# Two-layer decoder step on one core: the attention of layer 1 weighs its exponentials ahead of the value product, and collects the output as features by queries in one bank

## The chip, the cores and the metric

The program runs on one core of a Trainium2 chip. The metric is the device time of one launch in microseconds (us). TensorE is called PE here, VectorE DVE, ScalarE ACT, GpSimd POOL and SyncE SP, as the profile does. PSUM has eight banks of 512 fp32 columns per partition; the code calls them `PS[:, bank, :]`.

## What is computed

One step of a two-layer decoder trunk for a prompt of 512 tokens and 8 samples. Layer 1, which the change touches, is sparse attention with 16 query heads in 4 groups (one K/V head each). For the prompt it comes down to:

```python
o_c, p_c = cmp_attend(q, q_pos, blocks)        # 16 block means as keys
o_s = sel_attend(q_rot, q_pos, idx, rows)      # chosen 64-token blocks
o_w = win_attend(q_rot, q_pos, kv_w, k_pos)    # window of 512
gate = sigmoid(gts + b_gate)                   # 3 per head and query
o = gate[..., 0:1] * o_c + gate[..., 1:2] * o_s + gate[..., 2:3] * o_w
y = einsum('bte,ed->btd', o.reshape(B, T, NSA_W) * silu(z), w_out)
```

With 512 tokens there are 8 blocks and the top 16 are taken, so the selected branch is plain causal attention over its own K/V, as is the window branch. Each branch is a softmax of its own.

## The kernel before

Every projection is a tile of 128 output features by 520 columns (512 prompt tokens and 8 samples). `project` multiplies it with fp32 data split in a high and a low part: for each of 16 slices k of the contraction, three products (high by high, low by high, high by low) of two halves of 260 columns, six matmuls. ACT makes the high part of the weights (`split_hi`, `split_half`), POOL the low part (`split_lo`, four operations of 128x512 for a tile), and the weights come in by SP's queue, two tiles ahead. All layers together have some 145 such tiles.

Layer 1 goes through the 4 groups `g`, unrolled. A group has 14 tiles: 4 of queries, 6 of keys and values (with the samples' paged caches worked in between), and 4 of z, the output gate, one for each head `jj`. Beside the four z tiles stand the 16 **turns** n of the prompt's attention: `jj = n // 4` is the head, `i = n % 4` the block of 128 queries, and with i the number of key blocks grows from 1 to 4, for the selected (r = 0) and the window branch (r = 1). The engines are in-order queues with semaphores, the order is the code's. In turn n PE

- waits for the exponentials of turn n (`at_exp`), turns them (`T`, a multiplication with the identity; i + 1 blocks for each branch) into banks 4 and 5,
- multiplies the scores of turn n + 1 into banks 0 and 1 (`scores`), and runs 2 to 5 slices k of the z tile (`project(... part=...)`),
- turns back the combined output of turn n - 1 (`back`),
- in even turns 2 to 12 multiplies values of a sample's cache (`values`), whose sum DVE takes out (`d_vs`, awaited by the next turn's transposes),
- and multiplies the turned exponentials with the values of both branches and the compressed one, each into 128 columns of its own in bank 6 + n % 2: queries by features.

DVE in turn n copies the turned window part to SBUF, then adds the mask and takes the maxima of turn n + 1 (`maxima`), makes gate over sum for turn n (`weight`), copies the turned-back output of turn n - 1 (`backed`), takes out sample sums or the z tile, and adds the three products of turn n, each weighed by a number per query (`combine`). After a head, `gated` multiplies by silu(z). ACT copies the turned selected part, takes the exponentials of turn n + 1 with their sums (`expo`), and at the end of each head silu, with table loads; after `expo` in turns 4, 5, 8, 9, 12 and 13 it makes half of a tile's high part. POOL's four operations follow the second half.

In group 3 the splits of the output (`y_hi`, `y_lo`) for the output projection stand in turns 12 to 15 and behind them. The output projection's first tile waits for them slice by slice. `end_of_group` stands behind the first four slices of the tile that follows a group.

Of the kernel before, what the change touches and what calls it, by code (L numbers as in the profile page):

```python
# [18 lines left out]
ALU = mybir.AluOpType  # L19
AX = mybir.AxisListType.X  # L20

P = 128
D = 2048
KT = D // P
TP, NS = 512, 8
# [129 lines left out]
def trunk(nc, I, O):  # L155
    ctx = ExitStack()
    with ctx:
# [84 lines left out]
        weighed = few[:, 1024:1152], S1["pnb"]  # L242
# [558 lines left out]
        def _(pe):  # L801
# [195 lines left out]
            for g in range(4):  # L997
# [142 lines left out]
                def back(n, g=g):  # L1140

                    pe.wait_ge(S["at_cb"], 16 * g + (n + 1))
                    T(PS[:, 6 + n % 2, 384:512], weighed[n % 2], ident).then_inc(S["at_bk"], 1)

# [39 lines left out]
                for n in range(16):  # L1184
                    jj, i = n // 4, n % 4
                    pe.wait_ge(S["at_exp"], 16 * g + (n + 1))
# [27 lines left out]
                    if n >= 2:  # L1214
                        pe.wait_ge(S["at_be"], 16 * g + (n - 1))
                    to = 6 + n % 2
                    for s in range(i + 1):
                        M(PS[:, to, 0:P], lhsT=pt[:, 0, s * P:(s + 1) * P], rhs=vr[:, 0, s * P:(s + 1) * P],
                          start=(s == 0), stop=(s == i))
                    pe.wait_ge(S["at_ptb"], 16 * g + (n + 1))  # L1220
                    for s in range(i + 1):
                        M(PS[:, to, P:2 * P], lhsT=pt[:, 1, s * P:(s + 1) * P], rhs=vr[:, 1, s * P:(s + 1) * P],
                          start=False, stop=(s == i), skip_group_check=True)
                    if n == 0:
                        pe.wait_ge(S["a_ptc"], g + 1)
# [4 lines left out]
                def end_of_group(g=g, back=back):  # L1230

                    back(15)
                    pe.wait_ge(S["a_rd"], 2 * g + 2)
# [299 lines left out]
        def _(dve):  # L1533
# [282 lines left out]
            for g in range(4):  # L1816
# [127 lines left out]

                def combine(n):

                    w, ot, of = st[:, 6 + n % 2], weighed[n % 2], PS[:, 6 + n % 2]
                    dve.wait_ge(S["at_o"], 16 * g + (n + 1))
                    step(TS(ot, of[:, 0:P], w[:, 0:1], None, ALU.mult))
                    step(STT(ot, of[:, P:2 * P], w[:, 1:2], ot, ALU.mult, ALU.add))  # L1950
                    TT(ot, ot, of[:, 2 * P:3 * P], ALU.add).then_inc(S["at_cb"], 1); own.done("at_cb")

                def backed(n):

                    jj, i = n // 4, n % 4
                    if g == 0 and n == 0:
                        dve.wait_ge(S["x_saved"], 32)
                    dve.wait_ge(S["at_bk"], 16 * g + (n + 1))
                    CPR(XY[:, bass.ds(4 * g + jj, 1), i * P:(i + 1) * P], PS[:, 6 + n % 2:7 + n % 2, 384:512]
                        ).then_inc(S["at_be"], 1); own.done("at_be")  # L1960

                def gated(jj):
# [18 lines left out]
                step(ins)  # L1981
                dve.wait_ge(S["d_eT"], g + 1)
# [27 lines left out]
                for n in range(16):  # L2010
# [9 lines left out]
                    if n:  # L2020
                        if i == 3:
                            t = Tile(A_BASE, 10 + jj, g, 14)
                            dve.wait_ge(S["proj_done"], t.n + 1)
# [4 lines left out]
                    if g == 3 and n == 15:  # L2028
                        y_lo(dve, own, 1, range(4, 6))
# [77 lines left out]
```

## Time and profile before

| | |
|---|---|
| median of 3 runs | 2167.11 us (2166.88 to 2167.21) |
| profiled execution, its time | 2167.76 us |
| its span, first to last instruction | 2166.0 us |
| PE busy with matmuls | 2134.1 us, 99% |
| DVE busy | 881.6 us, 41% |
| ACT busy | 703.8 us, 32% |
| POOL busy | 761.4 us, 35% |
| granted TensorE clock, mean | 0.999 |

Busy times are sums of instructions over the span. An in-order engine that is busy 41% of the time can still keep another waiting, so the wait rows of single places count here, not the shares. In a timeline row the first number is the start, the second the time from the first start to the last end of a run of like instructions. One fp32 product of the code stands as two passes on PE, one transpose as one. The time of a matmul includes its way through the array, so starts, not ends, tell how closely they follow. A number like 2.53 us for two instructions that overlap is not their sum.

### The profile page before, as it was taken

What the parts mean: (1) busy time and instruction counts of PE and PEld (TensorE: products, weight loads), DVE (VectorE), ACT (ScalarE), POOL (GpSimd) and SP (SyncE); (2) the same over time, 40 slices, a digit from 0 to 9 for tenths busy, and PEclk for the clock granted to TensorE, in tenths of its full rate; (3) what the DMA queues carried; (4) which work ended last, traced back from release to release, by engine and by line L of the source; (5) the groups of instructions that cost most, each with busy time, mean ns of one, the idle gap of its engine ahead of it and who ended that gap; (6) DMA issues with size and microseconds to landing.
All of it is one profiled execution on the core that took longest, in us unless ns stands there. A gap on an engine that the chain in (4) does not pass through costs nothing. (4 is left out here: it accounts for less than half of the span.)

```text
span 2166.0 us, 43620 instructions
## 1 busy us (share of the span) xinstructions
PE 2134.1 (99%) x17971; PEld 2031.3 (94%) x17971; DVE 881.6 (41%) x1831; ACT 703.8 (32%) x983; POOL 761.4 (35%) x584
## 2 busy tenths in 40 slices
PE   8999999999999999999999999999999999999998
PEld 7999999989899899999889999899898999899998
DVE  6423225135351462134356532663346532664112
ACT  5212124232242342142234322442234322444223
POOL 2444433425334344444321243214331242223441
PEclk9999999999999999999999999999999999999999
DMA  7333555637556334455534344344634345333433
GB/s 256 93 98 88 178 156 128 189 97 188 152 130 185 98 98 123 139 178 165 158 103 123 99 128 132 106 115 109 164 105 123 99 125 134 100 102 99 121 103 109
DMA packets 455224, 281.17 MB, mean 130 GB/s; under 512 B 19224, under 2 KB 445784, under 8 KB 453747
## 3 DMA queue, kind: packets, MB, share of 16 engines
q1 hardware_dynamic: 455051, 278.73, 45.8%
q8 instruction: 125, 2.05, 0.4%
q14 instruction: 48, 0.39, 0.1%
HBM read 249.87 MB, written 45.99 MB: 137 GB/s over the span
## 5 line engine op out<-in xcount | busy, mean ns | idle before, releaser
L345 POOL TENSOR_TENSOR w_lo<-w_raw,w_hi 128x512 fp32r<-128x512 f32 (+1 forms) x580 | 761.2, 1343 | 1371.0 <-ACT w_hi L329 1029.0
L368 PE MATMUL ps<-h_hi,w_hi 128*128 128x260 f32 x4640 | 962.8, 289 | 7.3 <-DVE h_lo L460 7.2
L368 PE MATMUL ps<-h_hi,w_lo 128*128 128x260 f32 x4640 | 934.4, 283 | 0.0
L368 PE MATMUL ps<-h_lo,w_hi 128*128 128x260 f32 x4640 | 932.8, 283 | 0.0
L368 PEld LDWEIGHTS ps<-h_hi,w_hi 128*128 128x128 f32 x4640 | 717.9, 188 | 31.5 <-issue 17.0
L368 PEld LDWEIGHTS ps<-h_hi,w_lo 128*128 128x128 f32 x4640 | 713.8, 188 | 0.0
L368 PEld LDWEIGHTS ps<-h_lo,w_hi 128*128 128x128 f32 x4640 | 712.5, 188 | 0.0
L329 ACT ACTIVATE w_hi<-w_raw 128x2048 fp32r<-128x2048 f32 x132 | 251.9, 1909 | 519.8 <-PE ps L368 497.5
L432 DVE TENSOR_TENSOR scratch<-ps,rstd 128x520 f32<-128x520 f32 x48 | 33.6, 700 | 265.9 <-PE ps L368 265.3
L469 DVE TENSOR_TENSOR xy<-ps,x_res 128x520 f32<-128x520 f32 x32 | 22.4, 700 | 256.1 <-PE ps L368 253.5
L1461 ACT ACTIVATE scratch<-ps,scratch 128x128 f32<-128x128 f32 (+3 forms) x128 | 66.3, 523 | 125.5 <-DVE scratch L1933 125.1
L501 ACT ACTIVATE scratch<-xy 128x520 f32 (+1 forms) x32 | 20.4, 638 | 256.0 <-DVE xy L469 247.3
L1448 ACT ACTIVATE rstd<-ps 64x520 f32<-64x520 f32 x24 | 14.4, 602 | 207.2 <-PE ps L368 207.2
L1120 PE MATMUL ps<-scratch 128*128 128x128 f32 (+3 forms) x256 | 80.0, 435 | 0.0
L1900 DVE TENSOR_TENSOR scratch<-ps,scratch 128x520 f32<-128x520 f32 x16 | 11.2, 700 | 113.8 <-ACT rstd L1449 113.8
L388 ACT ACT_TABLE_LOAD x44 | 56.5, 1283 | 1.5 <-PEq L2093 0.7
L1120 PEld LDWEIGHTS ps<-scratch 128*128 128x128 f32 x256 | 41.1, 191 | 16.1 <-issue 11.0
L1819 DVE COPY scratch<-ps 128x512 f32<-128x512 f32 x32 | 22.1, 692 | 80.4 <-PE ps L1019 79.9
L1473 ACT ACTIVATE scratch<-ps 128x128 f32<-128x128 f32 (+1 forms) x64 | 28.0, 437 | 79.5 <-PE ps L1193 79.0
L1932 DVE TENSOR_REDUCE scratch<-ps 128x2 f32<-128x256 f32 (+1 forms) x64 | 52.8, 825 | 2.2
L1193 PE MATMUL ps<-c_common,scratch 128*128 128x128 f32 x320 | 45.7, 274 | 4.3 <-ACT scratch L1461 4.2
L1761 DVE SCALAR_TENSOR_TENSOR scratch<-scratch 128x256 f32<-128x256 f32 x64 | 48.4, 756 | 2.3
(363 smaller groups left out, 1760.6 us busy)
## 6 DMA issues: line engine op xcount, KB each, us to landing
w_raw<-in_w_in SPq DMA_DIRECT2D x113, 1024.0 KB, 5.8
w_raw<-in_w_out SPq DMA_DIRECT2D x32, 1024.0 KB, 5.9
scratch<-in_cache_kv_sel SPq DMA_DIRECT2D x256, 64.0 KB, 1.9
scratch<-in_cache_kv_win SPq DMA_DIRECT2D x128, 128.0 KB, 2.4
scratch<-in_cache_kv_cmp SPq DMA_DIRECT2D x256, 64.0 KB, 2.0
out_kvw_s<-in_cache_kv_win SPq DMA_DIRECT2D x24, 512.0 KB, 6.7
x_scratch<-xy SPq DMA_DIRECT2D x2, 4160.0 KB, 14.5
x_res<-x_scratch SPq DMA_DIRECT2D x32, 260.0 KB, 6.1
```

What stands on the lines that cost most here:

```text
L329: nc.scalar.activation(WH[:, t.p, :, n], WR[:, t.p, :, n], ACT.Copy).then_inc(S["w_hi"], 1); own.done("w_hi")
L345: ins = nc.gpsimd.tensor_tensor(WL[:, t.p, k:k + 4, 0:n], WR[:, t.p, k:k + 4, 0:n], WH[:, t.p, k:k + 4, 0:n].bitcast(F32), ALU.subtract)
L368: mm = nc.tensor.matmul(PS[0:m, bank + c, 0:HALF], lhsT=w[:, t.p, k, 0:m], rhs=h[:, k, c * HALF:(c + 1) * HALF], start=(k == 0 and x == 0) ...
L388: own.step(nc.scalar.activation(CELL[:], ones[0:1, 0:1], func))
L432: ins = nc.vector.tensor_tensor(halves(out), ps2(t), halves(RS[:]), ALU.mult)
L469: nc.vector.tensor_tensor(halves(XY[:, 2 * i + j, :]), ps2(t), halves(XR[:, j]), ALU.add).then_inc(proj_read[t.p], 1)
L1120: mm = M(PS[:, r, 0:(i + 1) * P], lhsT=qt[:, jj, i * P:(i + 1) * P], rhs=kT[:, r, 0:(i + 1) * P], start=True, stop=True)
L1193: mm = T(PS[:, 4 + r, s * P:(s + 1) * P], pr[:, 2 * (n % 2) + r, s * P:(s + 1) * P], ident)
L1461: ins = A(pr[:, 2 * (n % 2) + r, 0:L], PS[:, r, 0:L], ACT.Exp, bias=S1["st"][:, 4 + n % 2, r:r + 1], scale=SCALE, accum_out=S1["st"][:, n ...
L1473: A(pt[:, 0, 0:L], PS[:, 4, 0:L], ACT.Copy).then_inc(S["at_pta"], 1); own.done("at_pta")
L1761: STT(cb[:, b, c * HD:(c + 1) * HD], S0["vb"][:, b], KDW[:, c, b:b + 1], cb[:, b, c * HD:(c + 1) * HD], ALU.mult, ALU.add).then_inc(S["m_c ...
L1932: step(V.tensor_reduce(st[:, 2 + n % 2], PS[:, 0:2, 0:(i + 1) * P], AX, ALU.max))
```

## The change

`weight(n)` now also multiplies the exponentials of both branches by gate over sum, in place, in SBUF (two operations of 128 x (i + 1)·128), and tells `at_w`; PE's transposes wait for that instead of `at_exp`. It is called for the turn ahead, `weight(n + 1)` in turn n, and `weight(0)` ahead of the group's compressed softmax. In the value product stationary and moving sides change places: values stand, weighed and turned exponentials move, so the result is features by queries, and all branches of the four query blocks of a head add up in the 512 columns of one bank (6 + jj % 2). The compressed branch is one product of 512 columns at a head's start. `combine`, `back` and `backed` go away; `gated` reads the bank. `end_of_group` waits for `gated(3)`. In group 3 one of the output's splits moves ahead.

```diff
@@ TensorE, a turn
-                    pe.wait_ge(S["at_exp"], 16 * g + (n + 1))
+                    pe.wait_ge(S["at_w"], 16 * g + (n + 1))
...
-                        back(n - 1)
...
-                    if n >= 2:
-                        pe.wait_ge(S["at_be"], 16 * g + (n - 1))
-                    to = 6 + n % 2
+                    to = 6 + jj % 2
+                    if i == 0:
+                        if n == 0:
+                            pe.wait_ge(S["a_ptc"], g + 1)
+                        if jj >= 2:
+                            pe.wait_ge(S["a_yz"], 4 * g + jj - 1)
+                        M(PS[:, to, :], lhsT=S1["vzf"][:, jj], rhs=few[:, 0:TP], start=True, stop=False,
+                          skip_group_check=True)
                     for s in range(i + 1):
-                        M(PS[:, to, 0:P], lhsT=pt[:, 0, s * P:(s + 1) * P], rhs=vr[:, 0, s * P:(s + 1) * P],
-                          start=(s == 0), stop=(s == i))
+                        M(PS[:, to, i * P:(i + 1) * P], lhsT=vr[:, 0, s * P:(s + 1) * P], rhs=pt[:, 0, s * P:(s + 1) * P],
+                          start=False, stop=False, skip_group_check=True)
...
-                    M(PS[:, to, 2 * P:3 * P], lhsT=few[:, i * P:(i + 1) * P], rhs=S1["vzf"][:, jj],
-                      start=False, stop=True, skip_group_check=True).then_inc(S["at_o"], 1)
+                    mm.then_inc(S["at_o"], 1)
...
-                    back(15)
+                    pe.wait_ge(S["a_yz"], 4 * g + 4)
@@ VectorE
+                    for r in range(2):
+                        p = pr[:, 2 * (n % 2) + r, 0:(i + 1) * P]
+                        ins = TS(p, p, st[:, 6 + n % 2, r:r + 1], None, ALU.mult)
+                    ins.then_inc(S["at_w"], 1); own.done("at_w")
...
-                def combine(n):
-
-                    w, ot, of = st[:, 6 + n % 2], weighed[n % 2], PS[:, 6 + n % 2]
-                    dve.wait_ge(S["at_o"], 16 * g + (n + 1))
-                    step(TS(ot, of[:, 0:P], w[:, 0:1], None, ALU.mult))
-                    step(STT(ot, of[:, P:2 * P], w[:, 1:2], ot, ALU.mult, ALU.add))
-                    TT(ot, ot, of[:, 2 * P:3 * P], ALU.add).then_inc(S["at_cb"], 1); own.done("at_cb")
-
-                def backed(n):
...
                 def gated(jj):
...
-                    y = XY[:, bass.ds(4 * g + jj, 1), 0:TP]
-                    TT(y, y, XR[:, jj % 2:jj % 2 + 1, 0:TP], ALU.mult)
+                    TT(XY[:, 4 * g + jj, 0:TP], PS[:, 6 + jj % 2, :], XR[:, jj % 2, 0:TP], ALU.mult)
...
                 step(ins)
+                weight(0)
                 dve.wait_ge(S["d_eT"], g + 1)
...
                     if n < 15:
                         maxima(n + 1)
-                    weight(n)
+                    if n > 0 and i == 0:
+                        gated(jj - 1)
+                    if n < 15:
+                        weight(n + 1)
                     if g == 3 and n in (13, 14):
                         y_lo(dve, own, 1, range(2 * n - 26, 2 * n - 24))
...
                     if g == 3 and n == 15:
-                        y_lo(dve, own, 1, range(4, 6))
+                        y_lo(dve, own, 1, range(4, 7))
...
-                    combine(n)
...
                 if g == 3:
-                    y_lo(dve, own, 1, range(6, 10))
-                backed(15)
+                    y_lo(dve, own, 1, range(7, 10))
                 gated(3)
```

Line numbers of the rows that follow are those of each kernel's own file. DVE's queue at the start of a group's turns, before (L1978 is the last operation on the samples' new keys, L1983 the copy that PE's transposes of turn 0 wait for, L1988 the start of the compressed softmax):

```order
L1974 COPY scratch<-ps 128x256
L1975 TENSOR_TENSOR scratch<-ps,scratch 64x512
L1978 TENSOR_TENSOR scratch<-ps,scratch 128x32 x2
L1983 COPY scratch<-ps 128x128
L1988 TENSOR_TENSOR scratch<-ps,scratch 128x64 x4
```

And of the changed kernel:

```order
L1959 COPY scratch<-ps 128x256
L1960 TENSOR_TENSOR scratch<-ps,scratch 64x512
L1963 TENSOR_TENSOR scratch<-ps,scratch 128x32 x2
L1936 RECIPROCAL scratch<-scratch 128x2
L1937 TENSOR_TENSOR scratch<-scratch 128x2
L1942 TENSOR_SCALAR scratch<-scratch 128x128 x2
L1969 COPY scratch<-ps 128x128
L1974 TENSOR_TENSOR scratch<-ps,scratch 128x64 x4
```

`weight(0)`, four operations, now stands ahead of that copy and of the whole compressed softmax.

DVE's queue in turns 1 and 2, before, from the copy of the turned exponentials of turn 1 (L1930 to L1933 are `maxima`, L1940 and L1941 `weight`, L1550 `backed`, L1949 to L1951 `combine`):

```order
L2014 COPY scratch<-ps 128x256
L1930 TENSOR_TENSOR ps<-ps,scratch 128x128 x2
L1932 TENSOR_REDUCE scratch<-ps 128x2
L1933 TENSOR_SCALAR scratch<-scratch 128x2
L1940 RECIPROCAL scratch<-scratch 128x2
L1941 TENSOR_TENSOR scratch<-scratch 128x2
L1550 TENSOR_SCALAR xy<-ps 128x128
L1949 TENSOR_SCALAR scratch<-ps,scratch 128x128
L1950 SCALAR_TENSOR_TENSOR scratch<-ps,scratch 128x128
L1951 TENSOR_TENSOR scratch<-scratch,ps 128x128
L2014 COPY scratch<-ps 128x384
```

And of the changed kernel, the same two turns, to the sample sum that ends turn 2 (L2025):

```order
L2000 COPY scratch<-ps 128x256
L1926 TENSOR_TENSOR ps<-ps,scratch 128x128 x2
L1928 TENSOR_REDUCE scratch<-ps 128x2
L1929 TENSOR_SCALAR scratch<-scratch 128x2
L1936 RECIPROCAL scratch<-scratch 128x2
L1937 TENSOR_TENSOR scratch<-scratch 128x2
L1942 TENSOR_SCALAR scratch<-scratch 128x384 x2
L2000 COPY scratch<-ps 128x384
L1926 TENSOR_TENSOR ps<-ps,scratch 128x128 x2
L1928 TENSOR_REDUCE scratch<-ps 128x2
L1929 TENSOR_SCALAR scratch<-scratch 128x2
L1936 RECIPROCAL scratch<-scratch 128x2
L1937 TENSOR_TENSOR scratch<-scratch 128x2
L1942 TENSOR_SCALAR scratch<-scratch 128x512 x2
L2025 COPY rstd<-ps 128x128
```

The four operations of 128x128 are gone; the two in place (L1942) are between the maxima and the next turn's copy, and in turn 2 ahead of the sample sum.

PE's queue in turns 0 and 1, before, from the last slice of turn 0 (L1218 and L1222 are the value products, L1226 the compressed one, L1193 the transposes, L1120 the scores):

```order
L368 MATMUL ps<-h_hi,w_lo 128x260 x2
L1218 MATMUL ps<-scratch 128x128
L1222 MATMUL ps<-scratch 128x128
L1226 MATMUL ps<-scratch 128x128
L1193 MATMUL ps<-c_common,scratch 128x128 x4
L1120 MATMUL ps<-scratch 128x384 x2
```

And of the changed kernel:

```order
L367 MATMUL ps<-h_hi,w_lo 128x260 x2
L1213 MATMUL ps<-scratch 128x512
L1216 MATMUL ps<-scratch 128x128
L1220 MATMUL ps<-scratch 128x128
L1187 MATMUL ps<-c_common,scratch 128x128 x4
L1119 MATMUL ps<-scratch 128x384 x2
```

The compressed product moved ahead of the turn's value products and is four times as wide.

## Rows read from the trace of the kernel before

**Rows 1.** The page, busy time of engines: us, share of the span, instructions.

```profile
PE 2134.1 (99%) x17971; PEld 2031.3 (94%) x17971; DVE 881.6 (41%) x1831; ACT 703.8 (32%) x983; POOL 761.4 (35%) x584
```

**Rows 2.** The waits from 1100 us on: total, times, longest (us).

```profile
PE ps L1193 <- ACT scratch L1461: 4.2, 4, 1.1
```

**Rows 3.** Timeline of PE, group 0, turns 0 to 6: start, us, instruction.

```profile
1122.92 0.38 PE L1193 MATMUL ps<-c_common,scratch 128*128 128x128 f32 x2
...
1130.11 0.66 PE L1193 MATMUL ps<-c_common,scratch 128*128 128x128 f32 x4 [0.96 <-ACT scratch L1461]
...
1134.05 0.27 PE L1143 MATMUL ps<-c_common,scratch 128*128 128x128 f32 x1
1134.16 0.61 PE L1218 MATMUL ps<-scratch 128*128 128x128 f32 x4
...
1135.28 0.84 PE L1193 MATMUL ps<-c_common,scratch 128*128 128x128 f32 x6
...
1142.00 1.04 PE L1193 MATMUL ps<-c_common,scratch 128*128 128x128 f32 x8
...
1146.86 0.38 PE L1193 MATMUL ps<-c_common,scratch 128*128 128x128 f32 x2
...
1159.35 0.82 PE L1193 MATMUL ps<-c_common,scratch 128*128 128x128 f32 x6
```

**Rows 4.** Timeline of ACT: the last part of the exponentials of turns 2, 3, 4, 6.

```profile
1134.99 0.20 ACT L1461 ACTIVATION_READ_ACCUMULATOR scratch<-ps,scratch 128x1 f32 x1
...
1141.25 0.20 ACT L1461 ACTIVATION_READ_ACCUMULATOR scratch<-ps,scratch 128x1 f32 x1
...
1145.95 0.20 ACT L1461 ACTIVATION_READ_ACCUMULATOR scratch<-ps,scratch 128x1 f32 x1
...
1157.82 0.20 ACT L1461 ACTIVATION_READ_ACCUMULATOR scratch<-ps,scratch 128x1 f32 x1
```

**Rows 5.** Timeline of DVE, group 0, turns 0 and 2.

```profile
1122.05 0.27 DVE L1978 TENSOR_TENSOR scratch<-ps,scratch 128x32 f32<-128x32 f32 x2
1122.46 0.29 DVE L1983 COPY scratch<-ps 128x128 f32<-128x128 f32 x1
...
1133.90 0.17 DVE L1940 RECIPROCAL scratch<-scratch 128x2 f32<-128x2 f32 x1
1134.10 0.16 DVE L1941 TENSOR_TENSOR scratch<-scratch 128x2 f32<-128x2 f32 x1
...
1140.66 0.29 DVE L2038 COPY rstd<-ps 128x128 f32<-128x128 f32 x1
```

**Rows 6.** Timeline of DVE before the turns: products by a number per partition, SBUF to SBUF.

```profile
1115.78 0.29 DVE L1874 TENSOR_SCALAR scratch<-c_common,scratch 128x128 f32<-128x128 f32 x1
1115.98 0.35 DVE L1875 TENSOR_SCALAR scratch<-scratch 128x256 f32<-128x256 f32 x1
```

**Rows 7.** DVE's groups by form: count, busy us, mean ns, idle before.

```profile
L1668 DVE TENSOR_SCALAR scratch<-scratch 128x384 f32<-128x384 f32 x4 | 1.7, 421 | 0.1
```

**Rows 8.** Timeline of POOL and DVE near 1107 and 1118 us.

```profile
1107.29 2.53 POOL L345 TENSOR_TENSOR w_lo<-w_raw,w_hi 128x512 fp32r<-128x512 f32 x2 [9.06 <-ACT w_hi L329]
1107.44 1.16 DVE L1906 COPY scratch<-scratch 128x8 f32<-128x8 f32 x1
...
1118.21 5.01 POOL L345 TENSOR_TENSOR w_lo<-w_raw,w_hi 128x512 fp32r<-128x512 f32 x4 [5.90 <-ACT w_hi L329]
```

**Rows 9.** Timeline of group 3, turns 13 and 15: the output's splits beside POOL.

```profile
1942.65 1.43 DVE L460 TENSOR_TENSOR h_lo<-xy,h_hi 128x520 fp32r<-128x520 f32 x2
...
1943.35 0.20 ACT L1461 ACTIVATION_READ_ACCUMULATOR scratch<-ps,scratch 128x1 f32 x1
...
1944.71 4.99 POOL L345 TENSOR_TENSOR w_lo<-w_raw,w_hi 128x512 fp32r<-128x512 f32 x4 [21.22 <-ACT w_hi L337]
...
1960.05 6.31 DVE L460 TENSOR_TENSOR h_lo<-xy,h_hi 128x520 fp32r<-128x520 f32 x4
```

**Rows 10.** Timeline of POOL in turn 6.

```profile
1159.18 1.27 POOL L345 TENSOR_TENSOR w_lo<-w_raw,w_hi 128x512 fp32r<-128x512 f32 x1 [35.96 <-ACT w_hi L337]
```

More of the change, by code:

```diff
@@ L1138, in cmp_turn @@
                     mm.then_inc(S["a_ctT"], 1)
-                def back(n, g=g):
-                    pe.wait_ge(S["at_cb"], 16 * g + (n + 1))
-                    T(PS[:, 6 + n % 2, 384:512], weighed[n % 2], ident).then_inc(S["at_bk"], 1)
                 def values(s):
@@ L1213, in _, with end_of_group @@
                         sample_rows(range(4))
[L1214 to L1216 removed]
+                    to = 6 + jj % 2
[6 more added lines that the diff above has]
+                          skip_group_check=True)
                     for s in range(i + 1):
[L1218 to L1219 removed]
+                        M(PS[:, to, i * P:(i + 1) * P], lhsT=vr[:, 0, s * P:(s + 1) * P], rhs=pt[:, 0, s * P:(s + 1) * P],
+                          start=False, stop=False, skip_group_check=True)
                     pe.wait_ge(S["at_ptb"], 16 * g + (n + 1))
                     for s in range(i + 1):
[L1222 to L1225, printed above, removed]
[L1226 to L1227 removed]
+                        mm = M(PS[:, to, i * P:(i + 1) * P], lhsT=vr[:, 1, s * P:(s + 1) * P],
+                               rhs=pt[:, 1, s * P:(s + 1) * P], start=False, stop=(i == 3 and s == i),
+                               skip_group_check=True)
+                    mm.then_inc(S["at_o"], 1)
                 sample_rows(range(4, 6))
[L1230 to L1232 removed]
+                def end_of_group(g=g):
+                    pe.wait_ge(S["a_yz"], 4 * g + 4)
                     pe.wait_ge(S["a_rd"], 2 * g + 2)
@@ L1943, in weight, with gated @@
                             S1["gw"][:, bass.ds(12 * g + (3 * jj + 1), 2), i:i + 1], ALU.mult))
-                def combine(n):
-                    w, ot, of = st[:, 6 + n % 2], weighed[n % 2], PS[:, 6 + n % 2]
-                    dve.wait_ge(S["at_o"], 16 * g + (n + 1))
-                    step(TS(ot, of[:, 0:P], w[:, 0:1], None, ALU.mult))
-                    step(STT(ot, of[:, P:2 * P], w[:, 1:2], ot, ALU.mult, ALU.add))
-                    TT(ot, ot, of[:, 2 * P:3 * P], ALU.add).then_inc(S["at_cb"], 1); own.done("at_cb")
-                def backed(n):
-                    jj, i = n // 4, n % 4
-                    if g == 0 and n == 0:
+                    for r in range(2):
+                        p = pr[:, 2 * (n % 2) + r, 0:(i + 1) * P]
+                        ins = TS(p, p, st[:, 6 + n % 2, r:r + 1], None, ALU.mult)
+                    ins.then_inc(S["at_w"], 1); own.done("at_w")
+                def gated(jj):
+                    if g == 0 and jj == 0:
                         dve.wait_ge(S["x_saved"], 32)
[L1958 to L1962, printed above, removed]
+                    dve.wait_ge(S["at_o"], 16 * g + 4 * jj + 4)
                     dve.wait_ge(S["a_z"], 4 * g + jj + 1)
-                    y = XY[:, bass.ds(4 * g + jj, 1), 0:TP]
-                    TT(y, y, XR[:, jj % 2:jj % 2 + 1, 0:TP], ALU.mult)
+                    TT(XY[:, 4 * g + jj, 0:TP], PS[:, 6 + jj % 2, :], XR[:, jj % 2, 0:TP], ALU.mult)
                     CP(S1["zs"][:, jj:jj + 1], XR[:, jj % 2:jj % 2 + 1, TP:TA]).then_inc(S["a_yz"], 1)
@@ L2044, in _ @@
                            ).then_inc(S["a_rd"], 1); own.done("a_rd")
-                    if n > 0 and i == 0:
-                        gated(jj - 1)
-                    combine(n)
                 dve.wait_ge(S["a_rdT"], 2 * g + 2)
```

15 lines of the change are left out of this document (6 added, 9 removed).

## The prediction

> **What bounds the kernel now.** I read the busy shares first: PE is busy 99% of the span [rows 1], so whatever leaves PE's queue shortens the time, and whatever makes PE wait lengthens it one for one. Then the waits of the part that the change touches: PE waits there for one thing only, the exponentials, four times, 4.2 us in all [rows 2], once per group, in turn 1 [rows 3]. Then the timeline, for how near the other turns are to such a wait. I compare the start of PE's transposes with the end of the exponentials that they need [rows 3, 4]: turn 1 waits; turn 2 starts at 1135.28, and its exponentials ended at 1134.99 + 0.20 = 1135.19, so it has 0.09 us to spare; turn 3 has 1142.00 - 1141.45 = 0.55; turn 4 has 1146.86 - 1146.15 = 0.71; turn 6 has 1159.35 - 1158.02 = 1.33. Every group repeats this. So the exponentials of the first turns, where only 2 or 3 slices of projection stand between scores and transposes, are on the path already, though DVE is busy 41%.
>
> **What the change takes off PE.** 64 turns back. One costs the distance of its start from the next one's, 1134.16 - 1134.05 = 0.11 us [rows 3]. The compressed products keep their columns: four of 128 (two passes each of 0.11 us, 0.22 a turn) become one of 512 (two passes of four times 0.11 or slightly less, about 0.87). The value products keep count and columns. So PE's own work falls by 64 x 0.11 = 7.0 us, 7.3 with the compressed part; within a head three turns get 0.33 shorter and the first 0.5 longer.
>
> **What it adds ahead of the transposes.** `weight` now stands between exponentials and transposes. Reciprocal and small product stand 0.20 us apart each [rows 5]. The products in place: 128 columns take 0.29 us with the next one 0.20 behind, 256 take 0.35 [rows 6], 384 take 0.42 [rows 7]; 0.07 per 128 columns, so 512 take 0.49 (estimate). The second starts about 0.08 us before the first has ended, as in [rows 6]. With about 0.10 to get from ACT to DVE (I take it from the neighbouring starts) and the same last step to PE as before, the transposes start after the end of the exponentials by 0.10 + 0.40 + first + last + 0.05: 1.04, 1.17, 1.31 and 1.45 us for 128 to 512 columns, where before 0.05 would do.
>
> **Turn by turn, group 0.** From the start of one turn's transposes to the next:
>
> - Turn 1 to 2: before 1135.28 - 1130.11 = 5.17. Now exponentials end 1135.19 - 1130.11 = 5.08 after the start of turn 1, as they hang on PE's scores and not on what is removed, then 1.31: 6.39. **+1.2**.
> - Turn 2 to 3: before 6.72. Exponentials 1141.45 - 1135.28 = 6.17, then 1.45; and here the sample sum is queued behind the products in place, and the transposes of turn 3 wait for it too: +0.3 (L2038 of [rows 5]), where before it was done long ahead. 7.94. **+1.2**.
> - Turn 3 to 4: before 4.86. Exponentials 4.15; 0.25 of it was DVE still in `combine`; 3.90 + 1.04 = 4.94. **+0.1**.
> - Turns 0 and 1: `weight(0)` stands ahead of the copy that PE awaits and of the compressed softmax, which DVE goes through without a pause until the maxima of turn 1. L1978 ends at 1122.32. The reciprocal ends at 1122.53. The small product reads two operands from SBUF, and POOL is in its four operations until 1118.21 + 5.01 = 1123.22 [rows 8]. That such a DVE operation waits for the running POOL one shows at 1107.44: a copy of 8 columns took 1.16 us, until the first of POOL's (2.53 / 2 = 1.26 us each) was over [rows 8]. So it ends near 1123.30, the products in place at 1123.83, and the copy starts at 1123.86 instead of 1122.46 [rows 5]: 1.40 late. All of it reaches turn 1's exponentials (before: end at 1130.06, the wait's end in [rows 3]), which then need 1.17: 1130.06 + 1.40 + 1.17 = 1132.63 against 1130.11. **+2.5**. The wider compressed product lies in this wait.
> - Turns 4 to 15: the spare time is 0.7 to 2.5 us, about what `weight` wants. Where PE decides, a head gets 4 x 0.11 + 0.02 shorter; the first turns of heads 2 to 4 begin about 0.1 late, as turn 4, and turns 6, 10, 14 are at par (1.33 against 1.31). I book **-0.1** for the twelve turns: PE's saving, given back in these places.
>
> A group comes to 1.2 + 1.2 + 0.1 + 2.5 - 0.1 = **+4.9 us**, four of them +19.6.
>
> **Group 3** has the output's low parts (L460) behind `weight` in turns 13 and 14. Before, two of them ran at 1942.65 and took 1.43 [rows 9], just ahead of POOL at 1944.71. Now they come behind `weight(14)`: exponentials end at 1943.55, products in place end 1.36 to 1.4 later, 1944.94, when POOL has started or stands first in line. Beside POOL four of them took 6.31, 1.58 each [rows 9]. The transposes of turn 14 wait for a copy behind them. I take 1944.94 + 1.3 + 0.6 + 1.7 + 0.75 = about 1949.2, against 1945.3 + 0.3 that the other groups pay: +3.5 more than these (+1.5 if DVE gets in first). Turn 15: two more, 1.43, behind `weight(15)` and ahead of the sample sum: +1.5. At the end PE now waits at the fifth slice for `gated(3)`, which stands behind three low parts beside POOL, where before it waited piecemeal at later slices for the same low parts: +0.3. Together +5.3.
>
> **Sum**: +19.6 + 5.3 = +24.9 us. The profiled execution took 2167.76 with a span of 2166.0; the median of the runs is 2167.11, 0.65 below it. On the median: 2167.1 + 24.9 = **2192**.
>
> **The lock, by the Trainium skill.** The Trainium skill (SBUF — State Buffer, Who interferes with whom) says that DVE and GpSimd share a pair of ports, that a DVE operation on two SBUF tensors, or a single-source one in a two-port mode, takes it exclusively, and that who issues first blocks the other for the whole instruction. The 1.16 us copy agrees. By that rule the products in place, 128 of them, are all of the kind that can be caught, and turn 0 is where they are; where DVE comes first, POOL waits, and that costs nothing.
>
> **Rivals.**
>
> (1) *PE's saving carries, no new waits* (faster): `weight` would have to lie in spare time everywhere: -7.3 us, **2160**. It speaks for it that PE is 99% busy and DVE loses 256 operations; against it that turns 1 to 3 have 0, 0.09 and 0.55 us to spare [rows 3, 4] and cannot hide 1.2 to 1.5. It decides only if `weight` cost under 0.3 us. Chance 5%.
>
> (2) *The chain is about half as long as I make it*, say 0.6 us a turn, no lock in turn 0, low parts in time: group +1.9 rather than +4.9, group 3 +1: about +9, **2176**. 10%.
>
> (3) *The lock catches more turns.* In turns 6, 10 and 14 POOL starts 1159.18 - 1158.02 = 1.16 us after the exponentials end [rows 4, 10]; the second product in place should start 0.10 + 0.40 + 0.34 = 0.84 after it. The margin is 0.32. If it is lost, each of 12 turns waits up to 1.25 us more: +15, **2207**. 10%.
>
> (4) *No net change*: saving and waits cancel, within 4.3 us (0.2%) of 2167. It needs waits of 7 us in all, 1.8 a group, less than turns 2 and 3 alone give. 3%.
>
> The forecast itself has 72%, and its own spread is 2182 to 2200: 0.2 us of error in `weight` at 16 waiting places is 3.2, the lock in turn 0 (0.6 x 4) 2.4, group 3's race 2 to 3.5. With the cases around it the range is 2175 to 2204. Faster by over 0.2% (what a measurement can tell from no change): 0.06; within: 0.04; slower: 0.90.
>
> **What the profile after would show.** PE's busy time some 7 us less, no turning back, and PE's waits for DVE's products in place (they can appear as waits for DVE `scratch` at the transposes) of about 1.2 us or more at turns 1, 2 and 3 of every group; the copy ahead of turn 0 near 1.4 us later in its group, with a small product of 128x2 lasting about 0.7; in group 3 a wait of 3 us at turn 14. Wrong I would be if the transposes of turns 2 and 3 start within 0.5 us of their exponentials' end, or if the exponentials come earlier than 5.08 and 6.17 us behind the turn before, which would mean that `combine` had delayed them.

## The result and the profile after

The changed kernel takes 2199.07 us (median of 4 runs, 2197.93 to 2199.52) against 2167.11: ratio 1.0146, 95% interval 1.0134 to 1.0158, slower by 32.0 us. The forecast was 2192, range 2175 to 2204. The profiled execution has a span of 2197.3 us, 31.3 more than before, and a mean granted clock of 0.997.

The page's busy times, to set beside [rows 1]:

```profile
PE 2137.2 (97%) x17811; PEld 2019.7 (92%) x17811; DVE 841.0 (38%) x1703; ACT 704.1 (32%) x983; POOL 761.5 (35%) x584
```

DVE is 41 us less busy and PE has 160 instructions fewer, yet the kernel is slower: PE's share fell from 99 to 97%. PE's busy time did not fall by the removed 7 us; it rose by 3. Stretches at half clock (below) are part of that, but not most: experiment 3, whose mean clock is 0.999 again, still has 2135.1, and experiment 6, where the new waits are gone, 2125.4. So the time has to be looked for in PE's waits, from 1100 us on (total, times, longest), beside the one row of [rows 2] (the short ones, 0.6 us and less in total, are left out):

```profile
PE ps L1187 <- DVE scratch L1942: 13.5, 21, 1.4
PE ps L1187 <- DVE rstd L2025: 5.9, 4, 1.5
PE ps L1187 <- DVE scratch L2030: 4.7, 4, 3.7
PE ps L1187 <- DVE scratch L1969: 4.3, 4, 1.1
PE ps L367 <- DVE scratch L1952: 3.9, 1, 3.9
PE ps L1187 <- DVE scratch L2019: 1.5, 1, 1.5
```

All are waits for DVE. L1187 are the transposes. L1942 are the products in place, L2025 the sample sum queued behind them in turn 2, L1969 the copy ahead of turn 0, L2030 the copy of sample rows in turn 13, L2019 a sample sum in turn 14, L1952 the end of `gated(3)`. Together 33.8 us. The kernel before had the 4.2 of [rows 2] and one row more, which [rows 2] leaves out: PE waits for low parts at the end of group 3.

```profile
PE ps L368 <- DVE h_lo L460: 3.2, 3, 1.7
```

So about 26 us of the waits are new, not 30.

PE's timeline in group 0 (start, us, instruction, wait), to set beside [rows 3]:

```profile
1123.74 0.44 PE L1187 MATMUL ps<-c_common,scratch 128*128 128x128 f32 x2 [1.07 <-DVE scratch L1969]
...
1132.26 0.66 PE L1187 MATMUL ps<-c_common,scratch 128*128 128x128 f32 x4 [0.93 <-DVE scratch L1942]
...
1138.64 0.88 PE L1187 MATMUL ps<-c_common,scratch 128*128 128x128 f32 x6 [1.39 <-DVE scratch L1942]
...
1146.69 1.06 PE L1187 MATMUL ps<-c_common,scratch 128*128 128x128 f32 x8 [1.47 <-DVE rstd L2025]
...
1151.68 0.44 PE L1187 MATMUL ps<-c_common,scratch 128*128 128x128 f32 x2 [0.28 <-DVE scratch L1942]
```

Turns 1 to 4 each begin with a wait. From turn 1 to 2 it is 1138.64 - 1132.26 = 6.38 us (forecast 6.39), to turn 3 8.05 (7.94), to turn 4 4.99 (4.94). DVE's timeline at the same places:

```profile
1121.97 0.17 DVE L1936 RECIPROCAL scratch<-scratch 128x2 f32<-128x2 f32 x1
1122.17 0.67 DVE L1937 TENSOR_TENSOR scratch<-scratch 128x2 f32<-128x2 f32 x1
1122.87 0.48 DVE L1942 TENSOR_SCALAR scratch<-scratch 128x128 f32<-128x128 f32 x2
1123.39 0.29 DVE L1969 COPY scratch<-ps 128x128 f32<-128x128 f32 x1
...
1137.44 0.17 DVE L1936 RECIPROCAL scratch<-scratch 128x2 f32<-128x2 f32 x1 [1.43 <-ACT scratch L1457]
1137.64 0.16 DVE L1937 TENSOR_TENSOR scratch<-scratch 128x2 f32<-128x2 f32 x1
1137.84 0.75 DVE L1942 TENSOR_SCALAR scratch<-scratch 128x384 f32<-128x384 f32 x2
```

DVE is idle 1.43 us until the exponentials of turn 2 end, then runs `weight` in 1.15, and the transposes start 0.05 later, at 1138.64. In turn 0 the small product took 0.67 instead of 0.16: POOL was in its four operations until 1122.82, and the product ended at 1122.84. The other three groups show the same, 0.67 or 0.68.

Group 3, turns 13 and 14, is the other place. The timeline of POOL, DVE and PE, to set beside [rows 9]:

```profile
1966.18 0.75 DVE L1942 TENSOR_SCALAR scratch<-scratch 128x384 f32<-128x384 f32 x2
...
1966.86 5.86 POOL L344 TENSOR_TENSOR w_lo<-w_raw,w_hi 128x512 fp32r<-128x512 f32 x4 [21.37 <-ACT w_hi L336]
...
1966.97 3.39 DVE L459 TENSOR_TENSOR h_lo<-xy,h_hi 128x520 fp32r<-128x520 f32 x2
1970.39 0.68 DVE L2030 COPY scratch<-ps 8x512 f32<-8x512 f32 x1
...
1971.22 1.50 PE L1187 MATMUL ps<-c_common,scratch 128*128 128x128 f32 x6 [3.74 <-DVE scratch L2030]
1972.51 2.95 PE L1119 MATMUL ps<-scratch 128*128 128x512 f32 x4
```

The two low parts took 3.39 us instead of 1.43, with POOL's operations between them, and the copy behind them came late. A thing I had not expected is in the last two rows: six transposes in 1.50 us (0.82 to 0.88 elsewhere) and the scores in 2.95 (1.88 elsewhere). PE's clock had fallen. The windows of that place, and those of the end of the group (stretch; busy us of PE, PEld, DVE, ACT, POOL; granted clock; DMA share; GB/s):

```profile
1967.00:1971.00 4.00, 0.48 (x5) 0.29 (x3) 3.93 (x3) 1.72 (x3) 4.00 (x3) 1.00 0.00 0
1971.00:1975.00 4.00, 3.78 (x11) 2.46 (x11) 0.63 (x2) 0.49 (x1) 1.71 (x2) 0.57 0.00 0
1975.00:1979.00 4.00, 4.00 (x34) 3.76 (x33) 1.89 (x4) 1.38 (x4) 0.00 (x0) 1.00 0.00 0
...
1993.00:1997.00 4.00, 3.45 (x16) 3.45 (x17) 3.83 (x7) 2.06 (x4) 1.71 (x2) 0.50 0.52 154
1997.00:2001.00 4.00, 4.00 (x29) 4.00 (x29) 2.65 (x5) 0.49 (x1) 0.00 (x0) 0.81 1.15 312
```

Twice PE waited nearly 4 us and then ran at the 1.2 GHz level (0.50) for 3 to 5 us. PE's rows at the end of the group, the first behind the wait and the last of the slow stretch:

```profile
1993.55 0.80 PE L367 MATMUL ps<-h_hi,w_hi 128*128 128x260 f32 x2 [3.87 <-DVE scratch L1952]
...
1998.48 0.44 PE L367 MATMUL ps<-h_hi,w_lo 128*128 128x260 f32 x2
```

Pairs of slices' matmuls stand 0.43 us apart until 1998.48 and 0.24 after it: from 1993.55 on eleven distances took 4.93 us instead of 2.64, 2.3 more.

### The profile page after: what moved, and what is told of

Read it like the earlier page. It is cut to its first block and busy times, and to the rows that moved or that the text cites. A ratio compares the mean times of both kernels' runs of the same rounds, so it can differ in the third digit from the quotient of the medians.

```text
span 2197.3 us, 43028 instructions
## 1 busy us (share of the span) xinstructions
PE 2137.2 (97%) x17811; PEld 2019.7 (92%) x17811; DVE 841.0 (38%) x1703; ACT 704.1 (32%) x983; POOL 761.5 (35%) x584
## 5 line engine op out<-in xcount | busy, mean ns | idle before, releaser
L1187 PE MATMUL ps<-c_common,scratch 128*128 128x128 f32 x320 | 48.2, 282 | 29.8 <-DVE scratch L1942 13.5
L1187 PEld LDWEIGHTS ps<-c_common,scratch 128*128 128x128 f32 x320 | 35.4, 142 | 37.5 <-DVE scratch L1942 24.0
L2000 DVE COPY scratch<-ps 128x128 f32<-128x128 f32 (+1 forms) x64 | 31.4, 491 | 62.1 <-PE ps L1187 61.3
```

Source lines behind the costliest of these rows:

```text
L1187: mm = T(PS[:, 4 + r, s * P:(s + 1) * P], pr[:, 2 * (n % 2) + r, s * P:(s + 1) * P], ident)
L2000: CP(pt[:, 1, 0:L], PS[:, 5, 0:L]).then_inc(S["at_ptb"], 1); own.done("at_ptb")
```

## The experiments

Each ratio is to runs of the kernel before on the same chip (median 2167.35 for experiments 1 to 4, 2167.21 for 5 to 8). Where a difference to the changed kernel is given, it is to its 2199.07, which stands beside 2167.11.

**1. No weighing ahead of the transposes.** PE waits for the exponentials again, and the products in place are gone (so the output is not weighed).

```diff
-                    pe.wait_ge(S["at_w"], 16 * g + (n + 1))
+                    pe.wait_ge(S["at_exp"], 16 * g + (n + 1))
...
-                    for r in range(2):
-                        p = pr[:, 2 * (n % 2) + r, 0:(i + 1) * P]
-                        ins = TS(p, p, st[:, 6 + n % 2, r:r + 1], None, ALU.mult)
-                    ins.then_inc(S["at_w"], 1); own.done("at_w")
```

Expected:

> The changed kernel without the products in place: PE's transposes wait for the exponentials alone, as before, and the exponentials stay unweighed (gate and sum are left out of the output); all else, the product's orientation, the wide compressed product and the queues' order, is as changed. My theory (the time is lost in the chain from exponentials over weight to the transposes): turns 2 and 3 start within 0.1 us of the before's distance or earlier, what is left is PE's saving of about 7 us, against about 0.9 us a group from the small operations of weight(0) ahead of the copy, and about 3 us at the end of group 3: about 2166 us (2161 to 2171). Rival one, the product itself got slower on PE (its orientation, 512 columns at once): 2190 or more. Rival two, DVE and POOL block each other all over: also most of it gone, but then turns far from POOL's bursts would have shown no wait.

Measured: 2172.47 us, ratio 1.0021 (1.0012 to 1.0031). 26.6 of the 32 us are gone, so the weighing is the cause in the main. The expected 2166 was not reached, and the waits tell why:

```profile
PE ps L367 <- DVE scratch L1948: 3.9, 1, 3.9
PE ps L1187 <- DVE rstd L2021: 2.2, 4, 0.6
PE ps L1187 <- DVE scratch L1965: 2.2, 4, 0.5
PE ps L1187 <- DVE scratch L2026: 2.1, 1, 2.1
```

What is left are the small operations of `weight` (waits at turns 0 and 3) and group 3: the low parts are still in front of what PE awaits, turn 13 to 14 is 1.9 longer than before, 14 to 15 2.1, and the end, which waits 3.9 again, 1.2. Of the 2.1, 1.7 are PE's clock: behind the wait of 2.1 us at turn 14 the granted clock was 0.74 from 1945 to 1947 us and 0.50 from 1947 to 1949, and the exponentials of turn 15 ended 7.2 us after the transposes of turn 14 (5.5 in the other groups). The other groups are 0.4 to 0.7 us shorter each than before, where I had booked PE's whole saving, 1.8.

**2. The numbers, but not the products.** The wait stays, at the small product of `weight`; the two products in place are left out (the output is not weighed).

```diff
-                    step(TT(st[:, 6 + n % 2:7 + n % 2].rearrange("p o r -> p r o"),
+                    TT(st[:, 6 + n % 2:7 + n % 2].rearrange("p o r -> p r o"),
...
-                            S1["gw"][:, bass.ds(12 * g + (3 * jj + 1), 2), i:i + 1], ALU.mult))
-                    for r in range(2):
-                        p = pr[:, 2 * (n % 2) + r, 0:(i + 1) * P]
-                        ins = TS(p, p, st[:, 6 + n % 2, r:r + 1], None, ALU.mult)
-                    ins.then_inc(S["at_w"], 1); own.done("at_w")
+                            S1["gw"][:, bass.ds(12 * g + (3 * jj + 1), 2), i:i + 1], ALU.mult).then_inc(S["at_w"], 1); own.done("at_w")
```

Expected:

> As the run without weighing, but the transposes wait for reciprocal and small product (gate over sum), which are not applied (the output is unweighed). My theory: 0.5 us more at turns 1 and 2, about 0.7 at turn 3 (the sample sum is queued behind), next to nothing elsewhere, so about 1.6 us a group over the run without weighing: about 2172 us (2168 to 2177). If the products in place alone were the cost, it would equal the run without weighing.

Measured, in one run, so without an interval: 2176.37 us. Waiting for the reciprocal and the small product costs 3.9 us over experiment 1 (expected about 6: turn 3 came no later, since it waits for the sample sum in both), the products in place the other 22.7. The small ones alone are waited for in turns 1 and 2 only, the turns with nothing to spare:

```profile
PE ps L1187 <- DVE scratch L1937: 4.4, 8, 0.6
```

With the products it is turns 4, 8 and 12 too, and the sample sum and the copy behind them.

**3. Low parts behind what PE waits for.** In group 3 the splits of turns 13 and 14 move behind the copy of the sample rows, and the last three behind `gated(3)`. Nothing else changes.

```diff
                     if n < 15:
                         weight(n + 1)
-                    if g == 3 and n in (13, 14):
-                        y_lo(dve, own, 1, range(2 * n - 26, 2 * n - 24))
...
                            ).then_inc(S["a_rd"], 1); own.done("a_rd")
+                    if g == 3 and n in (13, 14):
+                        y_lo(dve, own, 1, range(2 * n - 26, 2 * n - 24))
...
-                if g == 3:
-                    y_lo(dve, own, 1, range(7, 10))
                 gated(3)
...
+                if g == 3:
+                    y_lo(dve, own, 1, range(7, 10))
```

Expected:

> The changed kernel with group 3's low parts (y_lo) behind what PE waits for: in turns 13 and 14 behind the copy and the sample sum, at the end behind gated(3). My theory: turn 14 and 15 start as in the other groups (10.55 becomes about 7.1, 11.06 about 7.9 us), the granted clock stays at 1.00 there, and PE's wait of 3.9 us at the end goes back to the 3 us that the kernel before has in pieces: 9 to 11 us less, about 2189 us (2186 to 2193). Rival, the waits of group 3 only hide others (PE waits there for the same thing anyway): under 3 us less.

Measured: 2189.73 us, ratio 1.0103 (1.0086 to 1.0120), 9.3 less than the changed kernel. That is group 3's own share. From turn 13 to 14 it gives back 3.4 us, from 14 to 15 2.6, and from turn 15 to the end 4.0; the last is 1.2 more than the change had cost there, because the kernel before also waits for low parts at that place (10.0 in sum; turn 0 of group 3 came 0.4 later in this execution). What PE waits for at the end now, and the windows of both places, where the clock stays up:

```profile
PE ps L367 <- DVE h_lo L459: 2.0, 2, 1.3
```

```profile
1968.00:1972.00 4.00, 3.72 (x22) 2.80 (x23) 3.85 (x6) 1.74 (x3) 4.00 (x4) 1.00 0.00 0
1984.00:1988.00 4.00, 2.61 (x19) 2.32 (x19) 3.90 (x4) 3.13 (x6) 4.00 (x4) 1.00 0.48 139
1988.00:1992.00 4.00, 3.27 (x27) 3.06 (x26) 3.83 (x6) 0.12 (x1) 0.28 (x1) 1.00 1.15 315
```

The same low parts beside the same POOL burst: with nobody waiting for what stands behind them they cost nothing from turn 13 to 14 (7.14 us, 7.13 in the other groups), and 0.5 from 14 to 15. The 13.5 us of waits for the products in place are untouched.

**4. Scores ahead of the transposes.** PE multiplies the scores of turn n + 1 as soon as the exponentials of turn n are done, while DVE weighs them; DVE takes the maxima of turn n + 1 ahead of the copy of the turned part.

```diff
+                    pe.wait_ge(S["at_exp"], 16 * g + (n + 1))
+                    if n < 15:
+                        scores(n + 1)
                     pe.wait_ge(S["at_w"], 16 * g + (n + 1))
...
                     mm.then_inc(S["at_T"], 1)
-                    if n < 15:
-                        scores(n + 1)
...
+                    if n < 15:
+                        maxima(n + 1)
                     dve.wait_ge(S["at_T"], 16 * g + (n + 1))
                     CP(pt[:, 1, 0:L], PS[:, 5, 0:L]).then_inc(S["at_ptb"], 1); own.done("at_ptb")
-                    if n < 15:
-                        maxima(n + 1)
```

Expected:

> The changed kernel with PE's scores of the next turn ahead of its transposes (they need only the end of the exponentials, not the weighing), and DVE's maxima ahead of the copy of the turned part, so that the scores' 0.4 to 1.8 us lie in the time of the weighing. My theory: turns 1, 2, 3 lose 1.2, 1.5 and 1.6 us each of their distance, turns 4, 8, 12 about 0.3: 4 to 5.5 us a group, 16 to 22 in all, about 2180 us (2176 to 2184). Rival (PE's own work grew): within 3 us of 2199.

Measured: 2168.41 us, ratio 1.0004 (0.9995 to 1.0014): 30.7 us less than the changed kernel, where I had expected about 19. It does more than cover `weight`. Turn 1 to 2 is 5.20 us again, but 2 to 3 is 5.63, less than before (6.72): the exponentials of the next turn no longer hang on the transposes and DVE's copy of them, so they end 3.3 us after the transposes of turn 1 instead of 5.08, and 3.8 after those of turn 2 instead of 6.20. The first three groups are 0.8 to 1.1 us shorter than before, 6.5 shorter each than in the changed kernel. Group 3 gains 5.2 more than these: its wait at turn 14 fell from 3.74 us to 1.59, the granted clock stayed at 1.00 behind it, and turn 14 to 15 took 6.61 us instead of 11.06. What is left, the largest rows:

```profile
PE ps L1119 <- DVE scratch L1970: 4.2, 4, 1.1
PE ps L367 <- DVE scratch L1953: 3.9, 1, 3.9
PE ps L1190 <- DVE scratch L2031: 1.6, 1, 1.6
```

The start of a group (L1970, the copy behind `weight(0)`), and group 3; 1.5 us more are the sample sum at turn 3. Behind the 3.9 us at the end the clock is down again (0.52 from 1961 to 1965 us).

**5. Both, and one wait later.** Experiments 3 and 4 together; the wait for that copy (`d_ptd`) moves from ahead of turn 0 to behind its scores.

```diff
-                pe.wait_ge(S["d_ptd"], g + 1)
                 for n in range(16):
...
                     pe.wait_ge(S["at_w"], 16 * g + (n + 1))
+                    if n == 0:
+                        pe.wait_ge(S["d_ptd"], g + 1)
```

Expected:

> Both repairs in one kernel: scores ahead of the transposes, low parts behind what PE waits for; the wait for the copy at a group's start also moves behind the first scores. If the two are independent, the second takes off the 9.3 us here too: 2168.4 - 9.3 = about 2159 us (2156 to 2162), faster than the kernel before, so that PE's saving of 7 us shows in the end. If PE waits for the same thing in both, less: 2163 or more. The moved wait gives at most 0.9 us a group, and I expect nothing of it, since the turn of the compressed softmax is awaited next.

Measured: 2163.49 us, ratio 0.9983 (0.9974 to 0.9992). Below the kernel before by 0.2%, 4.9 us less than experiment 4, where 9.3 had been the worth of the low parts alone. Moving them gave 3.4, 2.6 and 4.0 us from turn 13 to 14, from 14 to 15 and at the end in experiment 3; on top of experiment 4 it gives 1.8, nothing and 3.9, since the slack of the new order already takes up much of what the low parts delay. The two gains overlap, as the second reading of the expectation had it. At the start of the groups a new wait shows in place of the old one:

```profile
PE ps L1133 <- DVE scratch L1995: 3.3, 4, 0.9
...
PE ps L1191 <- DVE scratch L1971: 1.1, 4, 0.3
```

L1133 turns the compressed probabilities, which DVE finishes behind `weight(0)` (L1995 is their last operation).

**6. The start of a group too.** The copy that turn 0 awaits goes ahead of `weight(0)`; DVE takes the maxima of turn 1 ahead of the compressed softmax and weighs turn 1 within it; PE turns the compressed probabilities in turn 1 and adds their product in the third turn of a head. ACT's exponentials of turn 1 move ahead of the compressed ones with them. One bank for all branches is what makes the late product possible: it may come at any place of the sum.

```diff
-                weight(0)
                 dve.wait_ge(S["d_eT"], g + 1)
                 CP(S1["ptc2"].rearrange("p a b -> p (a b)"), PS[:, 4, 0:128]).then_inc(S["d_ptd"], 1)
                 own.done("d_ptd")
+                weight(0)
+                maxima(1)
...
-                    if i == 0:
-                        if n == 0:
+                    if i == 0 and jj >= 2:
+                        pe.wait_ge(S["a_yz"], 4 * g + jj - 1)
+                    if i == 2:
+                        if n == 2:
                             pe.wait_ge(S["a_ptc"], g + 1)
...
-                        M(PS[:, to, :], lhsT=S1["vzf"][:, jj], rhs=few[:, 0:TP], start=True, stop=False,
+                        M(PS[:, to, :], lhsT=S1["vzf"][:, jj], rhs=few[:, 0:TP], start=False, stop=False,
```

Expected:

> As the kernel with both repairs, and the group's start reordered: DVE takes the maxima of turn 1 and copies turn 0 ahead of the compressed softmax, weighs turn 1 in the middle of it, PE turns the compressed part in turn 1 and multiplies it in as a head's third turn. My theory (DVE's unbroken chain from weight(0) over the compressed softmax to the exponentials of turn 1 costs 2.0 us a group after the change): turn 1's transposes 2 to 3 us earlier, 1 to 2 us of it kept: about 2153 us (2150 to 2157). Rival: the chain only moves to turn 2's exponentials: within 1 us of the kernel with both repairs.

Measured: 2155.50 us, ratio 0.9947 (0.9933 to 0.9960), 11.7 below the kernel before and 43.6 below the changed one. Its page, and its longest waits:

```profile
PE 2125.4 (99%) x17811; PEld 2013.2 (93%) x17811; DVE 842.5 (39%) x1703; ACT 704.2 (33%) x983; POOL 760.7 (35%) x584
```

```profile
PE ps L367 <- DVE h_lo L459: 2.0, 2, 1.3
PE ps L1119 <- ACT scratch L1461: 0.6, 4, 0.2
```

PE is busy 8.7 us less than before: here the saving of the change (7.3 by the forecast) shows at last, with no wait longer than 0.2 us in the turns.

**7. Control: the same order on the kernel before.** Scores ahead of the transposes, maxima ahead of the copy, the wait for the first copy behind the scores; the old combining and turning back stay.

```diff
-                pe.wait_ge(S["d_ptd"], g + 1)
...
                     pe.wait_ge(S["at_exp"], 16 * g + (n + 1))
+                    if n < 15:
+                        scores(n + 1)
+                    if n == 0:
+                        pe.wait_ge(S["d_ptd"], g + 1)
...
                     mm.then_inc(S["at_T"], 1)
-                    if n < 15:
-                        scores(n + 1)
...
+                    if n < 15:
+                        maxima(n + 1)
```

Expected:

> The kernel before the change with the same reordering alone (scores ahead of the transposes, maxima ahead of the copy). There nothing stands between exponentials and transposes, so by my theory there is little to hide: the wait of 1.05 us a group in turn 1 hangs on the maxima, which come 0.3 us earlier: 0 to 2 us less, about 2166 us. If it gains 5 us or more, the gain of the scores-first kernel was not about the weighing.

Measured: 2165.87 us, ratio 0.9994 (0.9985 to 1.0003). Of its waits in the turns 1.7 us are left:

```profile
PE ps L1223 <- DVE scratch L2017: 1.7, 4, 0.4
```

So by removing these waits too the kernel before could get to about 2164 (an estimate: 2165.87 less 1.7). Experiment 6 is 8.7 below that. Of this, 1.2 us are the end of group 3, where experiment 7 still waits 3.2 us for low parts and experiment 6 waits 2.0; the other 7.5 are what the change is worth when nothing new is waited for (7.3 by the forecast).

**8. The products in place twice.** Two more with the factor 1.0 ahead of the real ones, each pair 0.5 to 0.9 us.

```diff
+                    for r in range(2):
+                        p = pr[:, 2 * (n % 2) + r, 0:(i + 1) * P]
+                        ins = TS(p, p, 1.0, None, ALU.mult)
+                    step(ins)
                     for r in range(2):
                         p = pr[:, 2 * (n % 2) + r, 0:(i + 1) * P]
```

Expected:

> The changed kernel with two more operations in place for each turn (a product with 1.0, same size, ahead of the weighing), so the suspected cost doubled; the output is unchanged. Longer by 0.6 to 1.0 us in turns 0 to 4, 8, 12, nothing in turns 5, 9, 13 (1.1 us to spare). In turns 6, 10, 14 the third and fourth operation come after POOL has started. If DVE and POOL exclude each other as in the 1.16 us copy, each of them waits for POOL's running instruction, and these turns get 2.5 to 3.5 us longer: about 2260 us (2245 to 2280). If they don't, these turns get 0.8 us longer like the others: about 2231 us.

Measured: 2268.45 us, ratio 1.0474 (1.0458 to 1.0490), as the reading with the lock has it (2260; 2231 without). Its four runs lie further apart than those of the other kernels: 2266.83 us at a mean granted clock of 0.988, 2266.64 at 0.987, 2270.07 at 0.985, 2273.15 at 0.984. Turn 6, DVE, POOL and PE:

```profile
1169.10 0.63 DVE L1942 TENSOR_SCALAR scratch<-scratch 128x384 f32<-128x384 f32 x2
1169.77 2.82 DVE L1946 TENSOR_SCALAR scratch<-scratch 128x384 f32<-128x384 f32 x2
...
1169.77 5.17 POOL L344 TENSOR_TENSOR w_lo<-w_raw,w_hi 128x512 fp32r<-128x512 f32 x4 [46.51 <-ACT w_hi L336]
...
1172.64 1.54 PE L1187 MATMUL ps<-c_common,scratch 128*128 128x128 f32 x6 [2.68 <-DVE scratch L1946]
```

The real products now begin with POOL's burst and take 2.82 us instead of 0.75: POOL's operations get in between. In the changed kernel's turn 6 they run from 1163.75 to 1164.50, the second from about 1164.08 (0.42 a piece), and POOL starts at 1164.42: 0.34 us to spare. Its transposes start 1.30 us after the exponentials end, as in turn 2, so the lock does not touch it; 0.6 us more is enough to lose that. And PE's clock falls behind this wait of 2.68 us:

```profile
1170.00:1172.00 2.00, 0.00 (x0) 0.00 (x0) 2.00 (x2) 0.00 (x0) 2.00 (x2) 1.00 0.43 124
1172.00:1174.00 2.00, 1.36 (x7) 1.36 (x8) 0.58 (x1) 0.00 (x0) 2.00 (x3) 0.54 0.77 227
```

It does not always. Turn 10 of the same group waits 2.68 us as well, and keeps its clock:

```profile
1203.89 0.87 PE L1187 MATMUL ps<-c_common,scratch 128*128 128x128 f32 x6 [2.68 <-DVE scratch L1946]
```

```profile
1202.00:1204.00 2.00, 0.11 (x1) 0.11 (x2) 1.84 (x2) 0.00 (x0) 2.00 (x3) 1.00 0.29 83
1204.00:1206.00 2.00, 2.00 (x11) 1.28 (x11) 0.56 (x1) 0.49 (x1) 2.00 (x2) 1.00 0.00 0
```

This run has eight waits of 2.68 us, two in each group, with the same instructions around them. Behind four of them the clock fell, and the next transposes came 10.26 to 10.44 us later; behind the other four it stayed at 1.00, and they came 8.84 or 8.85 us later. So the fall costs 1.4 to 1.6 us here, and the length of the wait alone does not decide whether it comes.

## Why the prediction was right, and where its terms were off

The mechanism was the one forecast: PE's saving did not reach the span, and `weight` went onto the path where the exponentials already were. By its own steps, in us (measured: distances between the starts of the transposes, group 1 against group 1 of before; group 0's rows above agree to 0.2; group 3's three rows against what group 1 pays at the same place):

| step | forecast | measured |
|---|---|---|
| turns 0 and 1 | +2.5 | +2.4 |
| turn 1 to 2 | +1.2 | +1.2 |
| turn 2 to 3 | +1.2 | +1.3 |
| turn 3 to 4 | +0.1 | +0.1 |
| turns 4 to 15 and on to the next group | -0.1 | +0.5 |
| a group | +4.9 | +5.6 |
| group 3, turn 14 | +3.5 | +3.4 |
| group 3, turn 15 | +1.5 | +3.1 |
| group 3, end | +0.3 | +2.8 |
| sum (4 groups and group 3) | +24.9 | +31.7 |

The span grew by 31.3; the first group came 0.4 earlier than before in the profiled execution.

The measured time lies within the range, but 7 us above the forecast, and 4 of these come from PE's clock, for which neither the sum nor the spread had a term. That they fitted into the range was luck.

- **The cost of `weight`** was sized right: exponentials' end to transposes 1.17 and 1.30 us for 256 and 384 columns, 1.03 for 128, forecast 1.17, 1.31, 1.04. (The terms given for turn 2 to 3 add to 7.92, not 7.94, and those for turn 14 in group 3 to 1949.3, which is 3.7 over the 1945.6 and not 3.5; neither changes the reading.) Experiments 1 and 2 show it as the cause of the groups' loss.
- **The lock in turn 0** was there: the small product ended 0.02 us after POOL's operation. The transposes of turn 0 came 1.2 late relative to the exponentials, not 1.4.
- **Turns 4 to 15** were mis-sized, +0.5 for -0.1 in each group. The wide compressed product lengthens the first turn of a head by 0.56 to 0.61, and the other three do not give back 0.33 each: turn 7 to 8 is 0.11 longer, because turn 8 begins with `weight` on the path like turn 4, turn 13 to 14 is 0.15 longer for the copy of the sample rows, 5 to 6 gives 0.23. This is 2.4 us of the miss. In experiment 1, where `weight` waits for nobody, 5 to 6 and 7 to 8 give 0.34 and 0.32: the sizes of PE's saving were right, the booking as carried was not.
- **Group 3's race** at turn 14 went as written: POOL started at 1966.86, DVE's low parts at 1966.97. **Turn 15 and the end** are the other 4 us of the miss, and it is nearly all the clock, which the forecast did not have. The order there was about as written: two low parts made the wait for the sample sum 1.5 us at turn 15, and at the end PE waited 3.87 us for `gated(3)` where the kernel before waits 3.2 in pieces, +0.7 for a forecast of +0.3. The clock: the exponentials of turn 15 came 7.85 us after the transposes of turn 14, where the other groups show 6.18, since scores and slices between ran at half speed (1.7 us), and 2.3 us more were lost behind the wait at the end. Experiment 3 gives 9.3 us back for moving the low parts alone, and shows granted clock 1.00 at both places. The three rows of the table sum to 9.3 too, but not row by row: experiment 3 gains 0.5 less at turn 15 and 1.2 more at the end.
- **The rivals.** The lock did not catch turns 6, 10 and 14, though the margin is as thin as the 0.32 us I gave (experiment 8). The half chain is excluded by the rows of turns 1 to 3. That PE's saving carries is false for this order of code and true for that of experiment 6.
- **A sign that failed.** PE's busy time was to be 7 us less and is 3 more. It falls only when the new waits are gone (2125.4 in experiment 6).
- **My expectations of the experiments** erred where I took two effects as independent: experiment 1 kept a loss in group 3 that I had put down to the weighing, experiment 4 also freed the exponentials and kept the clock up at turn 14, and experiment 5 could gain only once what both repairs offer.

The Trainium skill (TensorE: Matmul & The Clock Gate, HAM oscillation — how this bites in real kernels) says that a wait of PE can cost a second time, when the engine falls back to its lower clock and begins the next work slow. The traces agree: 0.57 and 0.50 granted behind the two long waits, 1.00 behind those of 1.5 us and less; behind the waits of 2.68 us of experiment 8 it went both ways.

What stays open: I did not try the kernel before with its group start rearranged like experiment 6; the 2164 for it is its time less its waits. What decides whether the clock falls behind a wait of 2 to 3 us is not shown. Nor does a run separate the wait at the end from the clock behind it.

## What to carry to other kernels

When an operation moves from behind a matrix product to ahead of it, the total of its engine's work matters little, and its place in the chain between two products much: 1.15 us of `weight` in a turn outweighed 41 us less DVE work, and the same operations cost PE next to nothing (no wait in the turns over 0.2 us, experiment 6) once it had the next turn's scores to do meanwhile and the group's start was ordered to match. So move the work of the bounding engine in the same edit, and look what the other queues hold ahead of each operation that is waited for, above all long ones that nobody awaits. In a sum of waits, look for single ones of 2 us and more: they can cost the clock as well, and with them the time differed more from run to run (experiment 8).

## What the runs showed of the hardware

- PE's granted clock stayed 1.00 through waits of 1.1 to 1.5 us in the changed kernel, and was at half behind its waits of 3.74 and 3.87 us, which then cost 1.7 and 2.3 us more, about half as much as the wait itself. In between both occur: it fell behind the wait of 2.07 us in experiment 1 and behind four of the eight waits of 2.68 us in experiment 8, and stayed at 1.00 behind the other four and behind one of 3.04 us.
- DVE and POOL with long runs of SBUF operations take turns: two low parts of 128x520 took 3.39 us instead of 1.43, POOL's four 5.86 instead of 4.99. Products in place of 128x384 took 2.82 instead of 0.75. Even an operation on 128x2 elements waits for POOL's current one (0.67 instead of 0.16), while the reciprocal just ahead of it, in the same burst, took its usual 0.17.
